# Exp's table fetched earlier, a gate moved, and four places for scores in the mixer of a hybrid decoder layer

## The reference, cut to what matters

```python
proj = h @ w_in[l]
q, k, v, z, xBC, dt_raw = jnp.split(proj, SPLIT_POINTS, axis=-1)
attn = moba_attention(partial_rotary(heads(q)), partial_rotary(heads(k)), heads(v))   # 8 heads of 64
#   with 256 tokens and blocks of 256: p = softmax(where(k_pos <= q_pos, q @ k.T * 64**-0.5, -inf)); out = p @ v
ssd = ssd_mixer(z, xBC, dt_raw, ...)                                                   # 16 heads of 64, 2 groups
#   per head: y = (CB * exp(segsum(dt*A))) @ (X*dt) + X*D_skip
#   y = y * silu(z); y = rms_norm of each group of 8 heads (512 columns)
x = x + concatenate([rms_norm(attn), ssd]) @ w_out[l]
```

## Time and profile before

| what | us |
|---|---|
| three runs without the profiler | 555.37, 555.49, 556.57; median 555.49 |
| the profiled execution, as timed | 558.14 |
| the span inside it, as traced | 556.4 |
| PE busy | 539.0 (97% of the span) |
| DVE, ACT, POOL busy | 434.2, 339.6, 68.6 |

### The profile page before, as it was taken

The page is one execution under the profiler, slowest core; times in us unless marked ns, Lnnn a source line. Parts: engine busy times, 40 slices in busy tenths (PEclk is TensorE's granted clock), DMA queues, the critical chain, the costliest instruction groups (busy, mean ns, idle before and its releaser), DMA issues.

```text
span 556.4 us, 9709 instructions
## 1 busy us (share of the span) xinstructions
PE 539.0 (97%) x3637; PEld 491.0 (88%) x3637; DVE 434.2 (78%) x657; ACT 339.6 (61%) x552; POOL 68.6 (12%) x104
## 2 busy tenths in 40 slices
PE   8999899999999989999999999999999999999994
PEld 6999799999999968998788678889999999999993
DVE  4899788888888695778667666589998888888845
ACT  6756466556555565866987874476566556556533
POOL 2003000000000330342542002000000000000015
PEclk9999999999999999999999999999999999999999
DMA  9866945556665327567526225345675566655302
GB/s 266 290 227 229 315 138 189 175 190 226 226 182 175 97 82 221 152 197 291 194 80 224 77 82 169 130 150 171 216 253 196 168 209 226 226 160 184 109 1 75
DMA packets 69966, 99.70 MB, mean 179 GB/s; under 512 B 1941, under 2 KB 55393, under 8 KB 69938
## 3 DMA queue, kind: packets, MB, share of 16 engines
q1 hardware_dynamic: 68336, 94.48, 51.8%
q0 software_dynamic: 1456, 4.59, 2.5%
q10 hardware_dynamic: 146, 0.27, 0.1%
HBM read 98.27 MB, written 1.06 MB: 179 GB/s over the span
## 4 chain that ended last, share of the span: by engine, by line
PE 78%; DVE 8%; ACT 5%; DMA 4%; issue 3%; POOL 1%; SPq 0%; POOLq 0%; DVEq 0%; ACTq 0%
PE bank L1600 24%; PE bank L1601 24%; PE bank L1602 24%; DMA raw<-in_ffn_w 4%; DVE w_lo L1079 2%; PE bank L1741 1%; ACT w_hi L632 1%; ACT decay L956 1%; DVE x L1096 1%; DVE mix_m L1466 1%; ACT decay L933 1%; POOL rstd L480 1%; PE bank L1884 0%; DVE hT_lo L1142 0%; PE bank L1886 0%
## 5 line engine op out<-in xcount | busy, mean ns | idle before, releaser
L1600 PE MATMUL bank<-hT_hi,w_hi 128*128 128x256 f32 x736 | 208.8, 284 | 2.4 <-DVE tok_rows L1247 2.3
L1601 PE MATMUL bank<-hT_lo,w_hi 128*128 128x256 f32 x736 | 208.2, 283 | 0.0
L1602 PE MATMUL bank<-hT_hi,w_lo 128*128 128x256 f32 x736 | 208.2, 283 | 0.0
L1079 DVE TENSOR_TENSOR w_lo<-raw,w_hi 128x1024 fp32r<-128x1024 f32 x128 | 158.2, 1239 | 25.5 <-ACT w_hi L632 25.0
L632 ACT ACTIVATE w_hi<-raw 128x1024 fp32r<-128x1024 f32 x128 | 134.0, 1054 | 42.8 <-PE bank L1602 26.1
L1600 PEld LDWEIGHTS bank<-hT_hi,w_hi 128*128 128x128 f32 x736 | 141.1, 192 | 5.5 <-DVE tok_rows L1247 3.7
L1601 PEld LDWEIGHTS bank<-hT_lo,w_hi 128*128 128x128 f32 x736 | 141.1, 192 | 1.5
L1602 PEld LDWEIGHTS bank<-hT_hi,w_lo 128*128 128x128 f32 x736 | 141.1, 192 | 0.0
L1600 PE MATMUL bank<-w_hi,hT_hi 128*128 128x512 f32 (+1 forms) x192 | 70.6, 368 | 1.3 <-DVE hT_lo L1142 0.7
L1602 PE MATMUL bank<-w_hi,hT_lo 128*128 128x512 f32 (+1 forms) x192 | 68.2, 355 | 0.0
L1601 PE MATMUL bank<-w_lo,hT_hi 128*128 128x512 f32 (+1 forms) x192 | 68.0, 354 | 0.0
(11 more groups left out here) (216 smaller groups left out, 804.7 us busy)
## 6 DMA issues: line engine op xcount, KB each, us to landing
raw<-in_ffn_w SPq DMA_DIRECT2D x54, 1024.0 KB, 5.4
raw<-in_w_in SPq DMA_DIRECT2D x16, 1024.0 KB, 5.6
tok_rows<-in_ffn_w SPq DMA_DIRECT2D x10, 1024.0 KB, 5.3
raw<-in_w_out SPq DMA_DIRECT2D x6, 1024.0 KB, 5.0
raw<-in_ffn_w SPq DMA_DIRECT2D x8, 256.0 KB, 5.1
x<-in_x SPq DMA_DIRECT2D x4, 256.0 KB, 4.0
norm_w<-cs_heads POOLq DMA_DIRECT2D x2, 512.0 KB, 4.7
out_x<-normed SPq DMA_DIRECT2D x3, 256.0 KB, 2.3
```

What stands on the lines that cost most here:

```text
L1079: dve.tensor_tensor(lo, src, hi, ALU.subtract).then_inc(half_ready, 1)
L1600: pe.matmul(dst, lhs[0], rhs[0], start=start, stop=False, skip_group_check=True)
L1601: pe.matmul(dst, lhs[0], rhs[1], start=False, stop=False, skip_group_check=True)
L1602: return pe.matmul(dst, lhs[1], rhs[0], start=False, stop=stop, skip_group_check=True)
```

## The change

Three things are changed, all in the mixer's loop, and no arithmetic of the result.

1. A one-element-wide Exp into an unused tile stands on ACT in step 19, ahead of the second `x_tok_out`. The table load for Exp moves with it.
2. `ssd_gate(0)` moves on DVE from step 24 (ahead of the split of half 29 and the matrices of heads 10 and 11) to step 25 behind them; `square_mix(4)` on ACT from step 25 to 26; `mix_scale(4)` on DVE from step 26 to 27.
3. Scores and probabilities have four places (decay and mix_m, two each). PE makes the scores of heads 0 to 3 after half 28, those of 4 and 5 between the two parts of half 30, those of 6 and 7 between the two parts of half 31. DVE takes the maxima of heads 0 to 3 in step 29, of 4 and 5 after the split in step 30, of 6 and 7 in step 31. ACT does exp of heads 2 and 3 after the splits of steps 29 and 30.

```diff
+        no_use = sb("no_use", [P, 1])
-        probs = decay
+        probs = [place[:, j, :] for place in (decay, mix_m) for j in range(2)]
@@ ACT
             def softmax_exp(h):
-                    act.activation(probs[:, h % 2, a:b], probs[:, h % 2, a:b], ACT.Exp,
+                    act.activation(probs[h % 4][:, a:b], probs[h % 4][:, a:b], ACT.Exp,
...
-                if 29 <= m < 32:
-                    softmax_exp(2 * (m - 29))
-                    softmax_exp(2 * (m - 29) + 1)
-                if m == 32:
-                    softmax_exp(6)
-                    softmax_exp(7)
+                if m in (29, 31, 32):
+                    h = {29: 0, 31: 4, 32: 6}[m]
+                    softmax_exp(h)
+                    softmax_exp(h + 1)
                 for split in splits(m):
                     mix_hi(split)
+                if m == 29:
+                    softmax_exp(2)
+                if m == 30:
+                    softmax_exp(3)
...
                 if m == 19:
+                    act.activation(no_use[:, :], minus_half[:, :], ACT.Exp)
                     x_tok_out(1)
...
-                if m == 25:
+                if m == 26:
                     square_mix(4, D_ATTN, 0)
@@ DVE
             def score_max(h):
                 dve.wait_ge(scores_done, h + 1)
-                if h >= 2:
-                    dve.wait_ge(probsT_done, h - 1)
-                s, kept = bank[:, score_bank(h), :], probs[:, h % 2, :]
+                if h >= 4:
+                    dve.wait_ge(probsT_done, h - 3)
+                s, kept = bank[:, score_bank(h), :], probs[h % 4]
...
-                if 29 <= m < 32:
-                    score_max(2 * (m - 29))
-                    score_max(2 * (m - 29) + 1)
-                if m == 32:
-                    score_max(6)
-                    score_max(7)
+                if m == 29:
+                    for h in range(4):
+                        score_max(h)
                 for split in splits(m):
                     mix_lo(split)
+                if m in (30, 31):
+                    score_max(2 * (m - 28))
+                    score_max(2 * (m - 28) + 1)
...
-                if m == 24:
+                if m == 25:
                     ssd_gate(0)
-                if m == 26:
+                if m == 27:
                     mix_scale(4, slice(D_ATTN, D_ATTN + 512), 4)
@@ PE
             def chunk_half(m):
                 chunk_part(m, 0)
+                if m in (30, 31):
+                    scores(2 * (m - 28))
                 chunk_part(m, 1).then_inc(half_used, 1)
...
-                if 28 <= m < 32:
-                    scores(2 * (m - 28))
+                if m == 28:
+                    scores(0)
+                    scores(2)
```

More of the change, by code:

```diff
@@ L1925, in probs_transposes @@
                     last = pe.transpose(bank[:, probs_bank(h), a * P:(a + 1) * P],
-                                        probs[:, h % 2, a * P:(a + 1) * P], ident)
+                                        probs[h % 4][:, a * P:(a + 1) * P], ident)
                 last.then_inc(probsT_done, 1)
```

## The result

The changed kernel takes 551.05 us (median of 4 runs, 550.53 to 551.42) beside 555.56 for the kernel before: 0.9909 of it, interval 0.9896 to 0.9921. By the ratio the gain is 5.1 us, by the medians 4.5. I forecast 3.5. In two later comparisons the ratio was 0.9914 (0.9901 to 0.9928) and 0.9888 (0.9849 to 0.9927). So the direction held, and some 1.6 us of gain came that my forecast did not have.

What follows compares the result with a forecast made beforehand. PE, busy 539.0 of 556.4 us, was taken as the bound. Terms 0.87 + 1.28 + 1.2 = 3.35 us, 3.7 followed step by step, were taken as 3.5: 555.49 - 3.5 = 552.0 us, range 551.0 to 553.9.

Steps and rivals of the forecast that it cites:

- Part 1: Exp's table load moved into ACT's idle stretch: PE's waits at SSD heads 0 and 3 go, gain 0.87 us.
- Part 2: First group's gate moved on DVE behind the matrices of heads 10 and 11: PE's wait at head 10 goes, 1.28 us.
- Part 3: Attention with reordered scores, maxima and exps: net gain 1.2 us, bounds from a loss of 0.2 to a gain of 1.6.
- The four waits: PE's attention waits, three for an exp and one for a row maximum: all go, 1.95 us gained.
- The wait for v: New PE wait at half 32's first product, until ACT has copied v out of its banks: 0.5 to 0.6 us lost.
- two more first products: In the attention, scores inside halves 30 and 31 cut each in two, adding restarts: 0.22 us lost.
- Together 4.1 us, the most that the change can give: Ceiling from PE's seven waits, each idle time plus 0.16 us: 2.15 at the SSD heads, 1.95 at the attention.
- The chain: Engines followed step by step to PE's transposes of heads 6 and 7: these come some 3.7 us earlier.
- A (ACT the bound): Rival: in the attention ACT's work slides and PE waits at v and scores 4; gain 2.3 us, 553.2; chance 0.15.
- B (POOL): Rival: POOL slows DVE's matrices in their new places, some SSD waits return; gain 2.8 us, 552.7; chance 0.12.
- C (nothing): Rival: the gain is given back ahead of the second SwiGLU by a transfer not there; 555.5 us; chance 0.03.
- D (slower): Rival: late copies of v hold PE at half 32; slower once that wait passes 3.9 us, 556.5; chance 0.04.

Runs made afterwards that it cites:

- table_again: The kernel before with only the early one-element Exp and its table load, run a second time: 554.02 us, ratio 0.9969 to the kernel before.
- table_behind: The changed kernel with the one-element Exp behind the second copy of the transposed x, not ahead of it: 552.5 us, ratio 0.9944 to the kernel before.
- gate_only: The kernel before with only the first group's gate, squares and scaling moved: 554.63 us, ratio 0.9968 to the kernel before.
- scores_only: The kernel before with only the four places and the new order of scores, maxima and exps: 554.23 us, ratio 0.9966 to the kernel before.
- tile_last: The changed kernel with the unused tile declared behind all other SBUF tiles: 551.71 us, ratio 0.9927 to the kernel before.
- tile_only: The kernel before with only the unused tile declared, ahead of the SwiGLU operands, and no instruction added: 555.76 us, ratio 1.0 to the kernel before.

## Why the prediction was right or wrong

**Part 1, right.** I took 0.87; the matched products give 0.53 at head 0 and 0.55 at head 3, 1.08 in all, table_again's whole stretch 1.18. That is a little above my upper bound of 0.87, since each wait cost more than I took. The load was hidden as said (copy of x at 261.68, load's end 261.55), and table_behind shows that the idle stretch is the reason.

**Part 2, right.** 1.28 forecast, 1.27 by the matched products, 1.31 by gate_only. The gate is cheaper in its new place (1.28 us for 1.82), and the heads, scaling and squares behind it made nobody wait.

**Part 3, the failed one: 1.2 forecast, 1.85 measured, above my bound of 1.6.** It had three terms. The four waits gave about 2.2 and not 1.95. The wait for v came where I said, for what I said, and idled 0.57 us as forecast. But its whole cost was 0.8 us: the six transposes in front of it and the wait take 317.33 - 315.95 = 1.38 us, where transposes with a half right behind them take 0.57. These two errors, 0.25 each way, cancel, which is luck.

The step that failed is "The scores inside halves 30 and 31 cut these in two, which is two more first products: 0.22 us". The new order switches more cheaply, not more dearly. Two pairs of scores in one group take 304.13 - 302.62 = 1.51 us where two groups of 0.85 would take 1.70. Six transposes with a half behind them take 307.56 - 306.99 = 0.57 us; I had priced all at the 0.75 that stood where scores followed. Summed over the attention the switches save about 0.4 us instead of costing 0.22 (what I expected of scores_only says 0.37, with 0.72 for the wait for v). That is 0.6 of the 0.65 by which the part was off.

**"Together 4.1 us, the most that the change can give" was wrong.** It was the sum of idle times and pipeline ends, and took the time of the products themselves for fixed. The mixer alone gave 4.26 even after the v wait took 0.8, and in the traces the tile another 0.6. My price of a wait, idle plus 0.16, was some 0.06 too low for the seven waits that went: over all of them I lacked 0.45 us (4.55 for 4.1). The first product behind a wait is longer too.

**What I had at nothing.** The declaration of `no_use` was no term of my sum, without a reason given. It is worth 0.6 us in the traces (tile_last, tile_only), though tile_only's times do not show it. The account of the traces: 3.35 of my sum + 0.2 (SSD waits) + 0.25 (attention waits) + 0.6 (switches) - 0.25 (v wait) = 4.15, measured 4.26; with the tile 4.9. The ratio's 5.1 (4.4 to 5.8) holds 4.9, and the mixer's 4.26 alone lies just below it; the later ratio 0.9914 (4.0 to 5.5) holds both.

**The chain and the sum.** Followed step by step I got 3.7 and from the terms 3.35, and took 3.5. The transposes of heads 6 and 7 were to start at 323.0 in the old trace's time; they start at 320.17, in a trace whose mixer starts 2.29 us sooner, so at 322.46. The 0.5 us more of gain go with the same terms, the switches above all.

**The rivals.** A (ACT the bound): no; no wait at the scores of 4 to 7, and ACT stood idle for 1.55 us, waiting for PE, before the copies of v. B (POOL): its mechanism is there and its price isn't. The matrices of heads 0 and 1 took 2.05 us and those of 10 and 11 1.61, where 1.40 is the undisturbed time. POOL was held up as well: its multiply took 1.50 us beside DVE's split at 267.84 and 0.53 the next time. But the spare of 0.6 and 0.5 us took it all, and no product waited. The rule of the Trainium skill that I weighed ("SBUF — State Buffer", section "SBUF: two separate sides", an exclusive lock for whole instructions) was to keep the first two waits by my reckoning. The trace agrees with it in so far as both engines are held up, 0.65 us and 0.97 us by these rows; that a hold-up of this kind makes PE wait it does not bear out. C (nothing): no; the three traces have no new wait of PE behind the mixer. D (slower): the place was right, and the wait stayed at 0.57 us, 0.8 with its restart, against the 3.9 that it needed.

**The range** ended where my account ended. I let it reach to the full 4.1 us, which I thought a ceiling, and the unpriced things lay beyond it.

## What to carry to other kernels

The sum of the idle times of the bounding engine is not a ceiling: when an order changes, price each switch between kinds of instruction by a row in which the same two kinds follow each other, also where the order removes such switches. A declaration is an edit as well: match the same instructions in both traces outside the changed stretch, test what is left with the declaration alone, and ask whether timed runs show it too. Load a table with a tiny instruction inside a stretch in which its engine waits anyway, since one place later it was worth nothing.

## What the runs showed of the hardware

- The place at which a tile of 4 bytes in each partition is declared changes the pace of PE's products in the traces: 118.98 us against 118.75 for the same products in the first SwiGLU. Most of it, 0.20 us, lies in the 63 products that read `gu_hi` and `gu_lo`. No timed comparison shows it clear of noise, and the cause is open.
- The granted clock can fall to 0.50, the 1.2 GHz level, for some three us behind a wait of PE of 1.1 us. It did in 2 of 9 traces that have this wait, at a cost of about 1.5 us. So a wait can cost more than itself; what decides whether it does is open.
- A table load lasts 1.28 us. The instruction before it on ACT ends at 260.26, the load starts at 260.27 and the next instruction at 261.57: no further time is lost on either side.
- A wait of PE costs more than its idle time: the one for v idled 0.57 us and cost 0.8. Six transposes take 0.57 us from their first to the start of a half behind them, and 0.75 when scores stand behind.
